# Both private weight tiles first, both shared weight tiles last: the order of the four up tiles of a mixture-of-experts block, and of their refills

## The reference, cut to what matters

```python
hup = xb @ w_up[e] + b_up[e]                      # (tokens, 1024) @ (1024, 2048)
glu = jnp.minimum(hup[:, 0::2], SWIGLU_LIMIT)
lin = jnp.clip(hup[:, 1::2], -SWIGLU_LIMIT, SWIGLU_LIMIT)
act = glu * jax.nn.sigmoid(SWIGLU_ALPHA * glu) * (lin + 1.0)
return act @ w_down[e] + b_down[e]                # (tokens, 1024) @ (1024, 1024)
```

## Time and profile before

| what | value |
|---|---|
| median of 3 runs | 1150.17 us (1147.97 to 1150.81) |
| the profiled execution, its own time | 1149.85 us |
| its span in the trace | 1148.1 us |
| PE busy | 1098.8 us, 96% of the span |
| DVE, ACT, POOL busy | 26%, 14%, 3% |
| granted TensorE clock | full, over the whole span |
| read from HBM | 432.01 MB |

### The profile page before, as it was taken

How to read it: one execution, slowest core, us unless ns; L and a number is a source line. 1 busy time by engine, 2 the same in 40 slices (tenths; PEclk the granted TensorE clock), 3 DMA queues, 4 the chain that set the end, 5 groups by cost and what they waited for, 6 DMA issues and landing times.

```text
span 1148.1 us, 14275 instructions
## 1 busy us (share of the span) xinstructions
PE 1098.8 (96%) x5292; PEld 447.5 (39%) x5292; DVE 298.5 (26%) x803; ACT 166.3 (14%) x343; POOL 34.1 (3%) x51
## 2 busy tenths in 40 slices
PE   8999999999999999999999999999999999999997
PEld 4467877633333333333333333333333333333332
DVE  5987244151121111111111111111111111111111
ACT  3042440121111111111111111111111111111110
POOL 5120010000000000000000000000000000000000
PEclk9999999999999999999999999999999999999999
DMA  7743487999999999999999999999999999999996
GB/s 216 192 140 66 152 266 270 412 372 393 430 428 428 428 428 428 427 429 429 429 429 428 429 428 427 428 428 428 429 429 428 429 429 429 429 427 428 426 428 261
DMA packets 63578, 435.13 MB, mean 379 GB/s; under 512 B 19856, under 2 KB 28096, under 8 KB 38592
## 3 DMA queue, kind: packets, MB, share of 16 engines
q1 hardware_dynamic: 57776, 433.17, 92.2%
q0 software_dynamic: 608, 1.34, 0.5%
q10 hardware_dynamic: 5168, 0.27, 0.3%
HBM read 432.01 MB, written 1.57 MB: 378 GB/s over the span
## 4 chain that ended last, share of the span: by engine, by line
PE 51%; DMA 39%; DVE 6%; SPq 2%; issue 1%; ACT 1%; DVEq 0%; ACTq 0%
DMA arena<-in_w_up 38%; PE bank L1064 23%; PE bank L1109 9%; PE bank L671 2%; PE bank L1008 2%; PE bank L617 2%; PE bank L993 2%; PE bank L947 2%; SPq L351 2%; PE bank L873 1%; DMA arena<-in_w_in 1%; PE bank L844 1%; PE bank L856 1%; PE bank L633 1%; PE bank L803 1%
## 5 line engine op out<-in xcount | busy, mean ns | idle before, releaser
L1064 PE MATMUL bank<-arena 128*64 128x512 f32 x2048 | 452.8, 594 | 30.8 <-DMA arena<-in_w_up 30.5
L1064 PEld LDWEIGHTS bank<-arena 128*64 128x64 f32 x2048 | 143.6, 137 | 332.7 <-issue 271.3
L1109 PE MATMUL bank<-arena 128*64 128x512 f32 x1024 | 226.8, 595 | 0.0
L1808 DVE TENSOR_SCALAR arena<-bank 128x256 f32<-128x256 f32 x64 | 27.2, 424 | 500.5 <-PE bank L1064 500.5
L1109 PEld LDWEIGHTS bank<-arena 128*64 128x64 f32 x1024 | 70.7, 137 | 133.9 <-issue 133.1
L1365 ACT ACTIVATE arena<-arena 128x256 f32<-128x256 f32 x64 | 26.6, 417 | 452.5 <-DVE arena L1809 452.5
L617 PEld LDWEIGHTS bank<-arena 128*128 128x128 f32 (+1 forms) x450 | 49.2, 143 | 89.2 <-issue 82.0
L617 PE MATMUL bank<-arena 128*128 128x128 f32 (+1 forms) x450 | 75.3, 290 | 8.5 <-DMA arena<-in_x 4.5
L1008 PE MATMUL bank<-arena 64*128 64x512 f32 x256 | 63.9, 616 | 0.7 <-ACT arena L1373 0.7
L993 PE MATMUL bank<-arena 128*64 128x512 f32 x248 | 60.1, 605 | 0.0
L633 PE MATMUL bank<-arena 128*128 128x512 f32 x128 | 57.9, 613 | 0.9 <-DMA arena<-in_w_in 0.9
(11 more groups left out here) (294 smaller groups left out, 517.0 us busy)
## 6 DMA issues: line engine op xcount, KB each, us to landing
arena<-in_w_up SPq DMA_DIRECT2D x125, 2048.0 KB, 25.5
arena<-in_w_down SPq DMA_DIRECT2D x63, 2048.0 KB, 26.8
arena<-in_w_in SPq DMA_DIRECT2D x16, 1024.0 KB, 5.8
arena<-in_w_up SPq DMA_DIRECT2D x5, 1024.0 KB, 7.7
arena<-in_w_out SPq DMA_DIRECT2D x4, 1024.0 KB, 6.4
arena<-in_w_proj_ssm SPq DMA_DIRECT2D x8, 256.0 KB, 5.2
arena<-in_w_proj_att SPq DMA_DIRECT2D x2, 1024.0 KB, 8.4
arena<-in_w_down SPq DMA_DIRECT2D x2, 1024.0 KB, 31.0
```

The costliest lines, as they stand in the source:

```text
L1064: last = pe.matmul(B[n][64 * h:64 * h + 64, :], xg[:, 2 * j + r, :], rows[r][2 * h + n], start=False, stop=(j == order[-1] and r == 1), sk ...
L1109: last = pe.matmul(B[3][64 * n:64 * n + 64, :], (actT_last if last_block else actT)[:, k % 4, k // 4, :], dn_w[parity][k // 4][:, k % 4, 5 ...
L1808: TS(part(glu_t, n), v[:, 0], LIMIT, None, ALU.min)
```

## The change

One tuple changes. `range(SHARED, UT)` is 2, 3 and `range(SHARED)` is 0, 1, so that blocks 1 to 29 take their up tiles as 2, 3, 0, 1 where they took 2, 0, 1, 3.

```diff
-        ORDER = (SHARED, *range(SHARED), SHARED + 1)
+        ORDER = (*range(SHARED, UT), *range(SHARED))
         ORDER_0 = (0, 2, 1, 3)
         ORDER_LAST = (*range(SHARED, UT), *range(SHARED))
```

## The result

The changed kernel is slower by a little: 1152.0 us median against 1149.24 us of the kernel before, 20 runs each, ratio 1.0025 with a 95% interval of 1.0019 to 1.0031. That is 2.8 us, under the 0.3% that one such measurement can tell and clearly above nothing with this many runs.

A forecast was written before the change was run, and what follows sets the result against it. The prediction took the always-full load queue (428 GB/s) as the bound. Steady blocks 0, block 30 +2.2 and block 31 +0.3 gave +2.5 us, 1152.7 us forecast; 8-in-10 range 1149.0 to 1155.8 us.

The forecast's parts named there:

- The steady blocks: Waiting blocks: tiles 0 and 1 are requested and needed 3.47 us later, period stays 29.37 us, price 0 per block.
- The hole in block 1: Block 2's tile 0 half and tile 1, requested one PE tile later into an empty queue, delay all later landings 3.46 us.
- Relief against delay, up to block 29: Up to block 29, landings 3.46 us later and needs 3.47 us later cancel, so PE's blocks start at the same times.
- A sign that fired: Block 30 starting earlier than 1088 would show the forecast wrong: the queue delay was not carried.
- The end: Blocks 30 and 31 keep their order, so delay without relief: +2.2 us in block 30, +0.3 us in block 31.
- Does a later margin swallow it?: At block 3's tile 0, requested 3.47 us later into a line 3.46 us longer: nothing changes.
- the frame: Block 2 to last load: queue never rests; early holes delay later landings, later requests that still find a line cost nothing.
- with nothing: -0.9 us: Lower bound with no queue delay: blocks 30 and 31 gain from PE's relief, -0.9 us, 1149.3 us median.
- The waits did not vanish: Rival: all PE waits on up tiles disappear, -30.5 us, about 1120 us; chance 0.03.
- The rate did not fall: Rival: bunched requests of each block cost transfer rate, over +3.45 us, some 1155 us; chance 0.20.
- No load landed ahead of one requested before it: Rival: tiles requested together share the queue, tile 1 up to 9.8 us late per waiting block, up to 1316 us; chance 0.01.
- The case of -0.9 us: Rival: a later pause in the queue swallows block 1's hole, -0.9 us, 1149.3 us; chance 0.15.

The follow-up runs named there:

- a longer hole: Changed kernel, but the second half of block 2's tile 0 also waits until all four up tiles of block 1 are used: 1154.01 us, ratio 1.0045.
- the two experiments that cured only the first: Changed kernel with block 1 kept at 2, 0, 1, 3 (1151.0 us, ratio 1.0017), or with block 1 taking 0, 1, 2, 3 (1150.09 us, ratio 1.0014).
- two of the kernels without either hole: Changed kernel with blocks 1 and 2 in old order (ratio 0.9996); kernel before with new order only in blocks 17 to 29 (ratio 0.9992).
- the combined one: Changed kernel with block 1 taking 0, 1, 2, 3 and blocks 2 and 3 in old order, requests following: 1149.12 us, ratio 1.0007.

## Why the prediction was right

**The time.** 1152.7 us were forecast, 2.5 over the run it started from; 1152.0 were measured, 2.8 over the kernel before. That the absolute numbers agree so well owes something to luck: the forecast started from a median of 3 runs, and that of 20 runs lies 0.9 us lower.

**The steady blocks** cost nothing, as forecast: period 29.36 us, the same waits one place further back, 428 GB/s. The experiments that put the new order only where a line stands (from block 3, from block 17) are not slower than the kernel before.

**The hole in block 1** opened where it was expected. Tile 1 of block 2 was requested at 278.13 and landed after 8.0 us, at 286.1; in the kernel before it landed at 283.3. With the block starts 0.67 us apart, that is 3.5 us, for 3.46 forecast. The load in the changed kernel:

```profile
L322 SPq DMA_DIRECT2D arena<-in_w_up x1: 328/328/328, 278.1 to 278.1; - x1
DMA to landing us min/median/max: 8.0/8.0/8.0
```

One block with the new order makes the loss by itself, and a longer hole makes it larger by the amount worked out.

**Relief against delay, up to block 29.** They were to cancel. In the two profiled executions they do so up to 0.8 us: block 10 starts 1.42 us earlier than before (509.51 against 510.93), of which 0.67 is the start of block 1. So less of the delay is left by then than was put in. It went at one load, a down tile of block 5. In the kernel before (first pair of lines) it lands at 363.3, in the changed kernel at 365.3:

```profile
L328 SPq DMA_DIRECT2D arena<-in_w_down x1: 333/333/333, 346.5 to 346.5; - x1
DMA to landing us min/median/max: 16.8/16.8/16.8
...
L328 SPq DMA_DIRECT2D arena<-in_w_down x1: 333/333/333, 345.8 to 345.8; - x1
DMA to landing us min/median/max: 19.5/19.5/19.5
```

The loads ahead of the two landed at 357.6 and 360.4. Against block 1 the changed kernel is 3.5 us late there, and 2.7 us late from this load on, since the kernel before took 5.7 us from one landing to the next and the changed one 4.9. Why is not known; the change does not touch it, and two executions of the same instructions differ by as much at block 10 (above).

**A sign that fired.** I had written that I would be wrong if block 30 started earlier than 1088. It started at 1087.03, 1.48 us earlier than before. Of this, 0.67 is the earlier start of block 1 and 0.8 the difference just told. The sign was set more tightly than single executions agree with each other, so it can neither confirm nor refute that the delay was carried; the landings do that.

**The end** went as worked out step by step: block 30 with two waits, 29.38 us instead of 27.10 (+2.3, forecast +2.2), and block 31 with a wait of 0.26 us (forecast 0.3). The final down tiles start 1.8 us later against block 1, not 2.5 (1135.07 in the changed kernel, 1133.93 before): the same 0.8 us are missing. That the order of block 30 decides over such an amount is shown by the run that takes it back.

**Where the reasoning was incomplete.** The step was "Does a later margin swallow it?". I worked out that block 3's tile 0 meets a line of 1.6 us and concluded, rightly for this kernel, that nothing changes, because the line is shifted as well. But under steady blocks I had written that the request finds a line as long as before, in every block, at a price of 0. In block 2 that is true only because the hole of block 1 had already been paid. Taken by itself the new order costs there too, 2.1 us by the medians of its own experiment and 2.6 by the ratio. The same run refutes a sentence of the frame, that a request which still finds a line ahead of it costs nothing by being later: this one had a line of 1.6 us in the kernel before. Two causes of similar size (3.7 and 2.6 us by the ratios of their own experiments) lay one behind the other, the later hidden by the earlier, and the two experiments that cured only the first found that out. The bound "with nothing: -0.9 us" was thus unreachable by curing the hole that I had seen.

**The rivals.** The waits did not vanish, as the full queue demanded. The rate did not fall. No load landed ahead of one requested before it, in either kernel's expert part. The case of -0.9 us is what two of the kernels without either hole come near to, 0.9996 and 0.9992, both with intervals that reach over 1; the third, the combined one, has 1.0007. That the relief alone makes the kernel faster is thus not shown.

## What to carry to other kernels

When a transfer queue is full for hundreds of microseconds, waits for it are no reserve: look instead for the place where it last ran dry, for a microsecond lost there comes out at the end, with no engine waiting anywhere near it. Before moving a request back, compare the shift with the line that each single request meets (time to landing less that of a lone load), in the first rounds above all, where the line is still building up, and leave a margin: a line that was 0.3 us longer than the shift still cost 0.9 us here. And cure a suspected cause by itself and also apply it by itself: here the cure alone looked like a refutation, because a second cause of the same kind stood behind the first.

## What the runs showed of the hardware that was not expected

A tile of 2 MB requested when the queue had run dry took 7.9 us from request to landing in the kernel before, 3.0 more than its share of the full queue's time (4.89 us). In other kernels of the study such a load took 7.8 to 8.7 us. The Trainium skill, DMA: Bandwidth & Descriptors, Anatomy of one DMA, gives about 2.0 us of fixed cost, for loads issued from GpSimd; here, with loads issued by SyncE, it is about 3.0, and the measurement decides.

How long a line a request meets differs between executions of the same code. Block 2's tile 1 landed 7.9 us after its request in the kernel before, and 9.6 us after it in the kernel that changes only block 30, although up to block 29 both run the same instructions and request it 10.6 us behind the start of block 1. So the price of a hole, read from one trace, is uncertain by up to 1.7 us here.

The profiled executions differ by up to 4 us in when block 1 starts (262.29 to 266.54), in code that is the same in all of them. This is more than most effects of this study, and why a single execution's span says little here.

Two things are not settled, and no experiment was made on either: why one load of the kernel before landed 0.8 us late with others in line ahead of it, and why a request that is out 4 us before the landing ahead of it still loses 0.5 to 1 us.
